# A hybrid decoder layer on one core: the z units ahead of the mLSTM values, norms in separate steps, Silu and gates later

## The reference

```python
p = split_cols(rmsnorm(x) @ w_in)
y_fox = fox_attention(fq, fk, fv, log_sigmoid(p['fox_f'] + fox_f_bias))       # 8 heads of 128
qkv = silu(causal_dwconv(p['gdn_qkv'], gdn_conv_w))                           # 4 taps
o_gdn = gated_deltanet(gq, gk, gv, sigmoid(p['gdn_b']), g)                    # chunks of 64, triangular solve
y_gdn = rmsnorm(o_gdn, gdn_norm_g) * silu(z)                                  # z = p['gdn_z'], norm per head
h = mlstm(mq, mk, mv, i_pre, ml_logf)                                         # chunks of 64, running maximum
y_ml = rmsnorm(sigmoid(p['ml_o']) * h, ml_norm_g)
y = g0 * (y_fox @ w_fox_proj) + g1 * (y_gdn @ w_gdn_proj) + g2 * (y_ml @ w_ml_proj)
x = x + y @ w_out
hid = causal_dwconv(rmsnorm(x) @ w_up, ffn_conv_w); out = rmsnorm(x + (silu(gt) * u) @ w_down)
```

## Time and profile before

| | before |
|---|---|
| median of 3 runs | 1882.47 us (1877.08 to 1885.93) |
| the profiled execution | 1882.46 us, its span 1880.7 us |
| TensorE busy | 1847.1 us |
| VectorE, ScalarE, GpSimd busy | 1066.6, 845.9, 457.3 us |
| mean granted TensorE clock | 0.990 |
| read from HBM | 321.45 MB, 172 GB/s |

### The profile page before, as it was taken

How to read it: one execution, slowest core, us unless ns; L and a number is a source line. 1 busy time by engine, 2 the same in 40 slices (tenths; PEclk the granted TensorE clock), 3 DMA queues, 4 the chain that set the end, 5 groups by cost and what they waited for, 6 DMA issues and landing times.

```text
span 1880.7 us, 27109 instructions
## 1 busy us (share of the span) xinstructions
PE 1847.1 (98%) x10325; PEld 1591.7 (85%) x10325; DVE 1066.6 (57%) x1271; ACT 845.9 (45%) x992; POOL 457.3 (24%) x242
## 2 busy tenths in 40 slices
PE   8999999999999999999999998999999999999997
PEld 6888899888877888888888887888888888888886
DVE  5666754355555575555555537666666666634334
ACT  5444443433553244444444445444444444444444
POOL 5212353211222022222222223222222222222223
PEclk9999999999999999999999999999999999999999
DMA  7545443344544355666667654666666656655553
GB/s 197 156 152 176 149 134 113 114 128 141 157 143 124 113 168 180 197 184 195 191 186 229 219 186 143 192 190 190 190 190 186 193 180 191 213 197 193 187 199 135
DMA packets 263433, 324.52 MB, mean 173 GB/s; under 512 B 16779, under 2 KB 230213, under 8 KB 262725
## 3 DMA queue, kind: packets, MB, share of 16 engines
q1 hardware_dynamic: 263366, 323.58, 56.3%
HBM read 321.45 MB, written 2.10 MB: 172 GB/s over the span
## 4 chain that ended last, share of the span: by engine, by line
PE 93%; DVE 3%; ACT 1%; issue 1%; POOL 1%; DMA 0%; DVEq 0%; SPq 0%; ACTq 0%; POOLq 0%
PE ps L560 92%; ACT w_hi L364 1%; DVE w_lo L369 1%; DVE acc L1583 0%; DVE xs L1758 0%; PE ps L818 0%; DMA x_in<-in_x_dram 0%; PE ps L841 0%; ACT x_sq L963 0%; PE ps L649 0%; POOL nlv L1877 0%; PE ps L623 0%; DVE x L1741 0%; DVE dmax L1441 0%; DVE pre L1318 0%
## 5 line engine op out<-in xcount | busy, mean ns | idle before, releaser
L560 PE MATMUL ps<-xnT,w_hi 128*128 128x512 f32 (+1 forms) x2960 | 1046.8, 398 | 4.8 <-DVE g_sum L1318 2.3
L364 ACT ACTIVATE w_hi<-raw 128x1024 fp32r<-128x1024 f32 x601 | 633.6, 1059 | 835.0 <-PE ps L560 830.4
L369 DVE TENSOR_TENSOR w_lo<-raw,w_hi 128x1024 fp32r<-128x1024 f32 x450 | 562.6, 1257 | 518.3 <-ACT w_hi L364 517.9
L560 PE MATMUL ps<-xnT,w_lo 128*128 128x256 f32 (+1 forms) x2960 | 826.6, 279 | 0.0
L369 POOL TENSOR_TENSOR w_lo<-raw,w_hi 128x1024 fp32r<-128x1024 f32 x151 | 370.1, 2451 | 1342.2 <-ACT w_hi L364 1342.0
L560 PEld LDWEIGHTS ps<-xnT,w_hi 128*128 128x128 f32 (+1 forms) x2960 | 559.2, 189 | 137.2 <-issue 3.7
L560 PEld LDWEIGHTS ps<-xnT,w_lo 128*128 128x128 f32 (+1 forms) x2960 | 560.1, 189 | 0.1
L560 PE MATMUL ps<-w_hi,xnT 128*128 128x512 f32 x1408 | 448.1, 394 | 1.9 <-DVE w_lo L369 1.9
L560 PEld LDWEIGHTS ps<-w_hi,xnT 128*128 128x128 f32 x1408 | 266.1, 189 | 56.8 <-DVE w_lo L369 2.0
L560 PE MATMUL ps<-w_lo,xnT 128*128 128x512 f32 x704 | 275.5, 391 | 0.0
L560 PEld LDWEIGHTS ps<-w_lo,xnT 128*128 128x128 f32 x704 | 133.2, 189 | 26.5
(11 more groups left out here) (326 smaller groups left out, 1178.2 us busy)
## 6 DMA issues: line engine op xcount, KB each, us to landing
raw<-in_w_in_dram SPq DMA_DIRECT2D x256, 512.0 KB, 3.7
raw<-in_w_up_dram SPq DMA_DIRECT2D x176, 512.0 KB, 3.8
raw<-in_w_down_dram SPq DMA_DIRECT2D x88, 512.0 KB, 4.3
raw<-in_w_out_dram SPq DMA_DIRECT2D x32, 512.0 KB, 4.6
raw<-in_w_fox_proj_dram SPq DMA_DIRECT2D x16, 512.0 KB, 3.4
raw<-in_w_gdn_proj_dram SPq DMA_DIRECT2D x16, 512.0 KB, 3.8
raw<-in_w_ml_proj_dram SPq DMA_DIRECT2D x16, 512.0 KB, 3.6
x_in<-in_x_dram SPq DMA_DIRECT2D x4, 512.0 KB, 5.8
```

The lines of the kernel that those rows point to most:

```text
L364: act.activation(w_hi[:, s, 0:n], raw[:, s, 0:n], ACT.Copy).then_inc(hi_ready[s], 1)
L369: eng.tensor_tensor(w_lo[:, s, 0:n], raw[:, s, 0:n], w_hi[:, s, 0:n], ALU.subtract).then_inc(lo_ready[s], 1)
L560: return pe.matmul(o, l, r, start=start, stop=stop)
```

## The change

- The two `z` units stand ahead of the two `mlv` units: z at chunks 113 to 128, mlv at 129 to 144. The tile `z` moves to another place in SBUF (that of `kbg`), and ScalarE waits for `wt` instead of `pv` before it writes it.
- The steps become two lists, one for ScalarE and one for VectorE, and are divided further: square, sum, mean, root, scale, gate. The gdn ones lie at chunks 116 to 125 (squares 116, 118; sums 117, 119; mean 120; root 121; scalings 123, 125), the products by z at 130 and 132, `gout` at 136 and 138. The ml ones lie at 168 to 175, `mout` at 178 and 179.
- ScalarE takes Silu of a `gdn` unit two chunks after the unit's end, behind the high parts of these chunks. `turn` items move by one chunk, the second `norm` by two.
- The feat transposes lie behind chunk 7, ScalarE's exponentials at 8, VectorE's second half (`scalar_decays`) at 9, `cumsum` at 12.
- The solve and what follows to the attention's `pv` move by one chunk. `mturn` stays at 116, now ahead of the second `fbc`. `vbc` lies at 136 and 138, `msel` to `sv` each one chunk later (`mbc` 147 and 149, `mqk` 149 and 151, `dc` 152 to 164, `sv` 158 and 166).

```diff
@@ UNITS
+UNITS += [("z", GDN_Z + 512 * g, g) for g in range(2)]
 UNITS += [("mlv", ML_V + 512 * g, g) for g in range(2)]
-UNITS += [("z", GDN_Z + 512 * g, g) for g in range(2)]
@@ plan_items
-    out = [(SMALL + 5, "cumsum", ())]
+    out = [(SMALL + 8, "cumsum", ())]
     for g in range(4, 12):
-        out.append((last_chunk("gdn", g) + 3, "turn", (g,)))
+        out.append((last_chunk("gdn", g) + 4, "turn", (g,)))
     out.append((last_chunk("gdn", 3) + 5, "norm", (0,)))
-    out.append((last_chunk("gdn", 7) + 5, "norm", (1,)))
+    out.append((last_chunk("gdn", 7) + 7, "norm", (1,)))
...
+    at += 1
     for lv in range(LEVELS):
...
+    gx = at + 1
...
-    out.append((last_chunk("mlqk", 3) + 4, "mturn", ()))
-    at = max(at, last_chunk("mlv", 1) + 1)
+    out.append((gx, "mturn", ()))
...
-    gy = last_chunk("z", 1) + 5
-    out += [(gy, "gout", (0,)), (gy + 1, "gout", (1,))]
+    gy = last_chunk("z", 1) + 2
+    out += [(gy + 6, "gout", (0,)), (gy + 8, "gout", (1,))]
     my = max(at, last_chunk("mlo", 1) + 1)
-    out += [(my + 13, "mout", (0,)), (my + 14, "mout", (1,))]
+    out += [(my + 10, "mout", (0,)), (my + 11, "mout", (1,))]
-    steps = [(gy - (15 if n < 5 else 7) + n, "gdn_out", n) for n in range(7)] + [(my + 2 * n, "ml_out", n) for n in range(6)]
+    act_steps = [(gx, "gdn_square", 0), (gx + 2, "gdn_square", 1), (gx + 5, "gdn_root", 0)]
+    dve_steps = [(gx + 1, "gdn_sum", 0), (gx + 3, "gdn_sum", 1), (gx + 4, "gdn_mean", 0), (gx + 7, "gdn_scale", 0),
+                 (gx + 9, "gdn_scale", 1), (gy, "gdn_gate", 0), (gy + 2, "gdn_gate", 1)]
+    act_steps += [(my + 1, "ml_square", 0), (my + 3, "ml_square", 1), (my + 5, "ml_root", 0)]
+    dve_steps += [(my, "ml_gate", 0), (my + 2, "ml_sum", 0), (my + 2, "ml_gate", 1), (my + 4, "ml_sum", 1),
+                  (my + 4, "ml_mean", 0), (my + 6, "ml_scale", 0), (my + 7, "ml_scale", 1)]
@@ tiles
-        z = part("z", 20, [P, NT, H, HD])
+        z = part("z", 12, [P, NT, H, HD])
@@ TensorE, chunk loop
-                if c == SMALL + 1:
+                if c == SMALL + 3:
                     pe.wait_ge(S["feat_ready"], 1)
@@ ScalarE, unit and chunk loop
                     if kind == "z" and g == 0:
-                        item_read(act, "pv", 1)
+                        item_read(act, "wt", 1)
...
-                if t == UNIT_CHUNKS[UNITS[u][0]] - 1:
+                if t == UNIT_CHUNKS[UNITS[u][0]] - 1 and UNITS[u][0] != "gdn":
                     unit(u)
-                if c == SMALL + 1:
+                if c >= 2 and UNITS[CHUNKS[c - 2][0]][0] == "gdn" and CHUNKS[c - 2][1] == 3:
+                    unit(CHUNKS[c - 2][0])
+                if c == SMALL + 4:
                     unit(None)
@@ VectorE
+            def scalar_decays():
+
+                sf = soft[:, :, :, :].rearrange("p t a h -> p (t a h)")
                 dve.wait_ge(S["soft_out"], 1)
...
-            def root_mean(r, root_in, root_done):
+            def mean_of(r, root_in):
...
+            def root_of(r, root_done):
+
                 dve.wait_ge(root_done, 1)
                 chain(dve.reciprocal(rstd[:, 2:4, :], rstd[:, 2:4, :]))
                 chain(tt_(rstd[:, 2:4, :], rstd[:, 2:4, :], r, ALU.mult))
...
+                elif name == "gdn_mean":
+                    dve.wait_ge(S["gsq_done"], 2)
+                    mean_of(rn[:, 0, :, :], S["groot_in"])
+                elif name == "gdn_scale":
+                    if n == 0:
+                        root_of(rn[:, 0, :, :], S["groot_done"])
+                    chain(tt_(gvt[:, n, :, :], gvt[:, n, :, :], over_free(rstd[:, 2 + n, :], HD), ALU.mult))
+                elif name == "gdn_gate":
+                    if n == 0:
+                        units_read(dve, "z")
+                    tt_(gvt[:, n, :, :], gvt[:, n, :, :], z[:, n, :, :], ALU.mult).then_inc(S["gy_ready"], 1)
...
-                if c == SMALL + 1:
+                if c == SMALL + 3:
                     scalar_gates()
+                if c == SMALL + 5:
+                    scalar_decays()
```

More of the change, by code:

```diff
@@ L144, in plan_items @@
         at += 4
-    gy = last_chunk("z", 1) + 5
-    out += [(gy, "gout", (0,)), (gy + 1, "gout", (1,))]
+    gy = last_chunk("z", 1) + 2
+    out += [(gy + 6, "gout", (0,)), (gy + 8, "gout", (1,))]
     my = max(at, last_chunk("mlo", 1) + 1)
-    out += [(my + 13, "mout", (0,)), (my + 14, "mout", (1,))]
-    steps = [(gy - (15 if n < 5 else 7) + n, "gdn_out", n) for n in range(7)] + [(my + 2 * n, "ml_out", n) for n in range(6)]
+    out += [(my + 10, "mout", (0,)), (my + 11, "mout", (1,))]
[5 more added lines that the diff above has]
+                  (my + 4, "ml_mean", 0), (my + 6, "ml_scale", 0), (my + 7, "ml_scale", 1)]
     order = sorted(range(len(out)), key=lambda k: (min(out[k][0], N1 - 1), out[k][0], k))
-    return [(min(out[k][0], N1 - 1), out[k][1], out[k][2]) for k in order], steps
-ITEMS, STEPS = plan_items()
+    return [(min(out[k][0], N1 - 1), out[k][1], out[k][2]) for k in order], act_steps, dve_steps
+ITEMS, ACT_STEPS, DVE_STEPS = plan_items()
 ITEM = {(name, args): k for k, (_, name, args) in enumerate(ITEMS)}
@@ L1134, in step @@
             def step(name, n):
-                if name == "gdn_out" and n < 2:
+                if name == "gdn_square":
                     if n:
@@ L1175, in _ @@
                     k += 1
-                for _, name, n in (e for e in STEPS if e[0] == c):
+                for _, name, n in (e for e in ACT_STEPS if e[0] == c):
                     step(name, n)
@@ L1618, in step @@
             def step(name, n):
-                if name == "gdn_out":
-                    tt = (n - 3) % 2
-                    o = gvt[:, tt, :, :]
-                    if n < 2:
-                        dve.wait_ge(S["gsq_in"], n + 1)
-                        dve.tensor_reduce(ss[:, 2 + n, :], osq[:, :, :], AX.X, ALU.add).then_inc(S["gsq_done"], 1)
-                    elif n == 2:
-                        dve.wait_ge(S["gsq_done"], 2)
-                        root_mean(rn[:, 0, :, :], S["groot_in"], S["groot_done"])
-                    elif n < 5:
-                        chain(tt_(o, o, over_free(rstd[:, 2 + tt, :], HD), ALU.mult))
-                    else:
-                        if n == 5:
-                            units_read(dve, "z")
-                        tt_(o, o, z[:, tt, :, :], ALU.mult).then_inc(S["gy_ready"], 1)
-                else:
+                if name == "gdn_sum":
+                    dve.wait_ge(S["gsq_in"], n + 1)
+                    dve.tensor_reduce(ss[:, 2 + n, :], osq[:, :, :], AX.X, ALU.add).then_inc(S["gsq_done"], 1)
+                elif name == "gdn_mean":
[9 more added lines that the diff above has]
+                    tt_(gvt[:, n, :, :], gvt[:, n, :, :], z[:, n, :, :], ALU.mult).then_inc(S["gy_ready"], 1)
+                elif name == "ml_gate":
                     if n == 0:
@@ L1637, in step @@
                         item_read(dve, "sv", NT - 1)
-                    if n in (1, 2):
-                        dve.wait_ge(S["msq_done"], n)
-                        chain(dve.tensor_reduce(ss[:, 1 + n, :], osq[:, :, :], AX.X, ALU.add))
-                    if n < 2:
-                        tt_(mv[:, n, :, :], mv[:, n, :, :], mo[:, n, :, :], ALU.mult).then_inc(S["msq_in"], 1)
-                    elif n == 3:
-                        root_mean(rd[:, :, :], S["mroot_in"], S["mroot_done"])
-                    elif n > 3:
-                        tt_(mv[:, n - 4, :, :], mv[:, n - 4, :, :], over_free(rstd[:, n - 2, :], HD), ALU.mult).then_inc(S["my_ready"], 1)
+                    tt_(mv[:, n, :, :], mv[:, n, :, :], mo[:, n, :, :], ALU.mult).then_inc(S["msq_in"], 1)
+                elif name == "ml_sum":
+                    dve.wait_ge(S["msq_done"], n + 1)
+                    chain(dve.tensor_reduce(ss[:, 2 + n, :], osq[:, :, :], AX.X, ALU.add))
+                elif name == "ml_mean":
+                    mean_of(rd[:, :, :], S["mroot_in"])
+                elif name == "ml_scale":
+                    if n == 0:
+                        root_of(rd[:, :, :], S["mroot_done"])
+                    tt_(mv[:, n, :, :], mv[:, n, :, :], over_free(rstd[:, 2 + n, :], HD), ALU.mult).then_inc(S["my_ready"], 1)
             for p in range(2):
@@ L1687, in _ @@
                     k += 1
-                for _, name, n in (e for e in STEPS if e[0] == c):
+                for _, name, n in (e for e in DVE_STEPS if e[0] == c):
                     step(name, n)
```

8 lines of the change are left out of this document (4 added, 4 removed).

## The result

Over 20 executions of each, the kernel before took 1888.07 us in the median (1875.88 to 1898.55) and the changed one 1878.3 us (1863.65 to 1881.73); the ratio is 0.9943 with a 95% interval of 0.9925 to 0.996. The change gains about 10 us; the forecast was 18.5 us, and 1878.3 lies above the range. The ratio is not the quotient of the medians (0.9948): by it the gain is 10.8 us, with 7.6 to 14.2 as its interval. Executions of one kernel differ by 18 to 23 us, far more than the 9 us of the three that were shown.

A forecast was written before the change was run, and what follows sets the result against it. TensorE, busy 1847.1 of 1880.7 us, was taken as the bound, leaving only its waits and clock dips. 1882.5 - 13.9 (waits) - 7.2 (clock) + 1.1 (new wait) + 1.5 (tight places) = 1864.0 us, range 1857 to 1876.

The forecast's parts named there:

- the tight places: Second gout transposes, gate 2's sum and msel, with little time to spare: 1.5 us allowed together, bounds 0 and 4.
- clock: Dips behind the removed waits at 94, 546, 578 and 672 us: 8.0 of missing clock, worth 7.2 us, bounds 0 to 7.7.
- the same to a few tenths: Claim that everything past 740 us stays the same to a few tenths.
- The Silu step: Convolutions: Silu two chunks later ends ScalarE's 6.6 us waits; gain 1.7 for the low-part wait at 88 us.
- The feat term: Scalar gates two chunks later: TensorE's wait for feat goes, gain 2.1 us, nothing from the clock.
- The mLSTM walks: Queues around mbc, mqk and mLSTM norm: low parts 152, 154 and g_sum in time; gate 2 nothing to about 1 us.
- The solve one chunk later: First solve item: one more chunk of 2.8 us covers its wait for nlv, gain 0.9 us.
- The new wait: Attention's softmax, behind p0 and p1: TensorE waits 1.1 us for low part 129, bounds none to 3.
- Rival (a): Waits go but dips stay, coming from work such as one-column products, also in mLSTM states: 1871 us, chance 0.20.
- (b): Waits move on to the mbc, mqk and gate items, half of 9.2 us comes back: 1871 to 1876, chance 0.15.
- (c): Softmax stretch turns serial, low parts late by 15 us over several chunks: slower, 1889 us, chance 0.05.
- (d): No new wait at all, waits of 13.9 and clock of 7.7 gained: 1861 us, chance 0.10.

The follow-up runs named there:

- after_again: The changed kernel run and traced once more, nothing edited; median 1875.21 us, ratio 0.993 to the kernel before.
- norm_split: Changed kernel with each norm item's 32 one-column products divided, 16 ahead of its chunk and 16 behind; 1868.34 us, ratio 0.9896 to the kernel before.
- root_late: Changed kernel with the delta-rule norm's root at chunk 126 instead of 121, scalings at 127 and 129; 1879.41 us, ratio 0.9956 to the kernel before.

## Why the prediction was wrong, point by point

**The level.** The sum stood against one execution, 1882.5, and a median of three. The kernel's median over 20 is 1888.07. Of the 14.3 us between 1864.0 and 1878.3, 5.6 lie here (1888.07 - 1882.5); the range allowed "some 4 us" for the scatter of a median. Had I asked how far two executions of the same program can lie apart behind 740 us, I would have had to leave some 9 us open.

**The gain.** The other 8.7 are a gain of 9.8 where 18.5 was forecast. From the traces (five of before, three of after, up to chunk 305):

| term | forecast | measured |
|---|---|---|
| waits, with the new one and the tight places | 13.9 - 1.1 - 1.5 = 11.3 | 13.0 - 4.0 = 9.0 |
| clock | 7.2 | (10.3 - 5.7) x 0.9 = 4.1 |
| pace in the gate stretch | 0 | -6.2 |
| sum | 18.5 | 6.9 |

The first two make 13.1, and the gain by chunk 190 is 12.8; with the third it is 6.9, and 6.6 by chunk 305. The timed executions say 9.8 by the medians and 10.8 (7.6 to 14.2) by the ratio; the 3 to 4 us between them and the traces stay unexplained. The traced executions of before are no fair sample: all five, 1874.93 to 1883.93 us, lie below its median of 1888.07, and no trace tells whether the others have the same pace in the gates. Some 2 us of scatter lie at the very start: the first chunk takes 3.7 us in some traces and 5.3 to 6.0 in others, whatever the kernel.

**Past 740 us, "the same to a few tenths".** This is the step that failed worst. The last item that the diff moves, mout, ends ahead of chunk 182, yet the gate stretch behind it goes at 2.83 us a chunk instead of 2.77, 6.2 us in all at a granted clock of 1.00 and without a wait. I had read the 0.35 us of the earlier trace rows as the one pace at full clock. The pace can change behind an item and is kept until the next; what in the program decides which it is stays open. That the order high, high, low, low removes both paces is shown, why is not.

**Waits.** Each step held where it named the wait: gvt, g_sum, m_t, feat and the low parts at 88 and 546 us left with their edits. The Silu step did what was said. Timeline of ScalarE in the changed kernel, for the earlier trace rows, and its waits from 60 to 220 us:

```profile
80.62 0.63 ACT L969 ACTIVATE wq<-acc 128x512 f32<-128x512 f32 x1 [0.17 <-DVE acc L1595]
```

```profile
ACT w_hi L370 <- PE ps L566: 72.9, 41, 3.6
...
ACT wq L969 <- DVE acc L1595: 0.2, 1, 0.2
```

A wait of 6.63 became 0.17, and what ScalarE now waits for is TensorE (72.9 us in 41 waits). The feat term was too large: 2.1 in the trace I had, 0.8 in the four others. It is 2.1 to 2.2 in the traces whose first chunk was slow, and 0.8 where it was not. The mLSTM walks held: no wait at mbc, mqk, mout or gate 2, against 1.5 allowed.

**The solve one chunk later** gained nothing. nlv's 0.9 went, and 1.2 for xm came. Timeline of the changed kernel: VectorE, GpSimd, TensorE.

```profile
244.99 3.14 DVE L1386 TENSOR_TENSOR xm<-ident,pm 128x1024 f32<-128x1024 f32 x1
...
244.64 2.40 POOL L375 TENSOR_TENSOR w_lo<-raw,w_hi 128x1024 fp32r<-128x1024 f32 x1 [1.79 <-ACT w_hi L370]
...
248.27 0.91 PE L566 MATMUL ps<-xm,nlv 128*128 128x128 f32 x6 [1.22 <-DVE xm L1386]
```

"Later solve items keep their spacing" is true among themselves, but not against GpSimd's low part of every fourth chunk: xm's step fell on one and took 3.14 us instead of 1.2. I had seen this very collision in the earlier trace rows and used it for the mLSTM norm only.

**The new wait** came where it was said, behind p0 and p1, for low part 129. Timeline of the changed kernel: TensorE's p0, VectorE's low part and scaling, TensorE behind the wait; the last row is TensorE in `after_again`, one chunk later.

```profile
492.29 0.27 PE L752 MATMUL ps<-ident,p 128*128 128x128 f32 x1
...
496.95 1.22 DVE L375 TENSOR_TENSOR w_lo<-raw,w_hi 128x1024 fp32r<-128x1024 f32 x1
498.08 3.42 DVE L1643 TENSOR_TENSOR gvt<-gvt,rstd 128x1024 f32<-128x1024 f32 x1
...
498.31 0.47 PE L566 MATMUL ps<-w_hi,xnT 128*128 128x512 f32 x1 [1.81 <-DVE w_lo L375]
...
499.71 0.50 PE L566 MATMUL ps<-w_hi,xnT 128*128 128x512 f32 x1 [1.52 <-DVE w_lo L375]
```

Probabilities 4.7 us behind p0's start where the walk had 4.2, the low part at 5.9 where it had 5.3, the wait 1.8 for 1.1. A dip of 1.7 us of missing clock follows (498 to 504 us), which I had kept for the bound. The two further traces of after have no dip there, but a second wait of 1.5 us, for low part 130. The second scaling stands ahead of that low part in VectorE's queue, beside GpSimd's low part 131, and takes 3.42 us instead of 1.2; in the first trace the slowed TensorE hid it. So the place costs 3.3 us where 1.1 was forecast, and the collision that the walk left out makes about half of it.

**Clock.** The step counted 8.0 of missing clock behind the waits that go, from one trace. Over five traces of before the sum of all dips is 8.5 to 13.7, mean 10.3; I had the highest. Each dip comes short (1.7 to 1.8) or long (3.4 to 3.5) or not at all, from one execution to the next. At the first norm it was short in four of five traces of before, with the wait ahead of it, and long in all three of after, without it: "long because of the wait" fell, and with it the 1.7 counted there. The two norms together miss 4.4 to 4.5 us in the mean of either kernel. All of the gain lies behind 480 us, where before misses 3.3 to 8.6 us, mean 5.8, and after 0 to 1.7, mean 1.1. Rival (a) was so far right: the dip at the first norm comes from the work, as `norm_split` shows. A dip without any wait also stands in 8 of the 18 traces somewhere between 594 and 648 us, behind a `dc` item, of whose matmuls 32 in the trace have one column (642 to 648 us in the first trace of before); it comes and goes from one execution to the next, as (a) had it for the mLSTM states. The dips behind gvt's, g_sum's and the low part's waits went with them (1.00 over 572 to 580 us above).

**The rivals.** (b) did not come: no wait moved on to mbc, mqk or the gates. (c) did not either: the softmax stretch holds 1.8 to 3.3 us of wait, not 15. (d) had the right clock at full price and no wait; neither held. None had a change of pace, and the range was made of these five cases alone. Two of their sums are loose by less than 1 us: in (b) 4.6 + 1.7 is 6.3, not 6.5; in (c) the clock without gvt's dip and the three short dips come to (8.0 - 2.9) x 0.9 = 4.6 each, not 3.8 and 4.8, so (c) comes to 1888.

**The table loads.** Timeline of ScalarE in the changed kernel:

```profile
468.21 1.06 ACT L370 ACTIVATE w_hi<-raw 128x1024 fp32r<-128x1024 f32 x1 [1.66 <-PE ps L566]
469.28 1.28 ACT L969 ACT_TABLE_LOAD   x1
470.58 1.03 ACT L969 ACTIVATE z<-ps 128x1024 f32<-128x1024 f32 x1
```

In the trace four loads of 1.28 us stand at chunks 116 to 125. The first starts at 469.28, 0.01 us behind the end of the high part before it, and Silu of z starts 1.30 us behind that, as in the earlier trace rows: there is no room for a drain on either side. The waits there are 1.8 to 3.3 us; the 5.5 us more that the Trainium skill's figures ("ScalarE: Activation LUTs", section "What ACT_TABLE_LOAD costs") would give it did not appear.

## What to carry to other kernels

Take the sum against a median of many executions, and ask for two or three traces of the kernel before: waits and dips that only one shows are scatter (feat 2.1 or 0.8, missing clock 8.5 to 13.7). When TensorE is 98% busy, read the starts of its matmuls in a stretch that the change doesn't touch: a pace 2% slower costs as much there as all waits together, and looks like full clock and no wait. Before an item or a step is moved by one chunk, lay GpSimd's work beside it: a step of VectorE on 128 x 1024 elements that falls on it takes 3 us instead of 1.2. That happened here three times (xm, the second scaling, the low part in `root_late`).

## What the runs showed of the hardware

- Alternating 512- and 256-column matmuls, each with its own weights, run at one of two paces at a granted clock of 1.00: 693 or 707 ns for four (2.773 or 2.827 us a chunk). The pace holds until small matmuls of an item, or in three traces a wait of 2.3 us, stand between two chunks, and can be the other one behind them; in the gates it is the same in all traces of a program (5 of before, 3 of after), in the MLP it changes from one execution to the next. Two of each kind by turns take 697 ns in all five kernels with that order (2.787 us a chunk), and the spread of executions of the kernel before falls from some 17 to 24 us to 7.8.
- The granted clock falls from 1.00 to 0.50 behind 32 one-column products in a row without any wait: 3.64 us of them at the second norm, 4.84 at the first in the changed kernel. The same products in two halves of 1.84 us, a chunk apart, leave it at 1.00 in two traces of two. The whole row brings the dip in all 16 traces at the first norm and in 13 of 16 at the second.
- A VectorE tensor_tensor of 128 x 1024 takes 3.14 to 3.43 us instead of 1.2 when one of GpSimd's has started before it, and GpSimd's stays at 2.4 to 2.6: 481.42 + 2.38 + 1.2 is 485.0, where VectorE's ended at 484.9, and 244.64 + 2.40 + 1.2 is 248.2 for 248.1. So VectorE waits for the whole of it and then does its own. The Trainium skill, "SBUF — State Buffer", section "SBUF: two separate sides", says the same of operations with two inputs in SBUF (an exclusive lock, the second one fully blocked); the trace agrees.
